# A decoder trunk on one core: the key lookup's small tensors move to the accumulation banks, and the modulation tiles run in quarters

## What is computed

```python
def adaln_params(c, w, b):
    return jnp.split(jax.nn.silu(c) @ w + b, 6, axis=-1)

def peer_ffn(h, w_q, sub_keys, u_tab, v_tab):
    ...
    v1, i1 = lax.top_k(s[:, :, 0], PEER_TOPK)
    v2, i2 = lax.top_k(s[:, :, 1], PEER_TOPK)
    cand = (v1[..., :, None] + v2[..., None, :]).reshape(n, PEER_HEADS, PEER_TOPK * PEER_TOPK)
    cidx = (i1[..., :, None] * PEER_N_KEYS + i2[..., None, :]).reshape(n, PEER_HEADS, PEER_TOPK * PEER_TOPK)
    best, sel = lax.top_k(cand, PEER_TOPK)
    eidx = jnp.take_along_axis(cidx, sel, axis=-1)
    gates = jax.nn.softmax(best, axis=-1)
    ...
```

## Time and profile before

| | us |
|---|---|
| median of 3 runs | 2521.32 |
| lowest, highest | 2515.03, 2521.76 |
| profiled execution, its own time | 2514.56 |
| its span | 2512.7 |
| TensorE busy in the span | 2400.0 |
| VectorE, ScalarE, GpSimd busy | 1419.9, 983.2, 634.3 |

### The profile page before, as it was taken

How to read it: one execution, slowest core, us unless ns; L and a number is a source line. 1 busy time by engine, 2 the same in 40 slices (tenths; PEclk the granted TensorE clock), 3 DMA queues, 4 the chain that set the end, 5 groups by cost and what they waited for, 6 DMA issues and landing times.

```text
span 2512.7 us, 51051 instructions
## 1 busy us (share of the span) xinstructions
PE 2400.0 (96%) x19142; PEld 2185.7 (87%) x19142; DVE 1419.9 (57%) x3306; ACT 983.2 (39%) x1645; POOL 634.3 (25%) x445
## 2 busy tenths in 40 slices
PE   7888999999999999999989977999999999999998
PEld 2478887888889999999978445899999999999998
DVE  6674269577778533333344232269988995333333
ACT  3334433333333344444443131444344434444443
POOL 1015457500000122222254000468500001222222
PEclk8989999999999999999999988999999999999999
DMA  6524455545454454454453663444433334554444
GB/s 246 196 68 152 142 167 187 181 161 168 160 168 143 143 186 162 164 166 167 161 207 117 233 237 136 155 151 159 134 126 126 130 129 135 185 167 165 162 165 144
DMA packets 114871, 405.45 MB, mean 161 GB/s; under 512 B 13275, under 2 KB 13403, under 8 KB 113723
## 3 DMA queue, kind: packets, MB, share of 16 engines
q1 hardware_dynamic: 111048, 388.68, 46.1%
q10 hardware_dynamic: 3699, 15.08, 1.5%
HBM read 394.58 MB, written 9.14 MB: 161 GB/s over the span
## 4 chain that ended last, share of the span: by engine, by line
PE 68%; issue 20%; POOL 9%; DMA 1%; ACT 1%; DVE 1%; POOLq 0%; ACTq 0%; DVEq 0%; SPq 0%
PE ps L1325 11%; PE ps L1329 11%; PE ps L1333 11%; POOL ring_lo L1968 8%; PE ps L1188 7%; PE ps L1189 7%; PE ps L1192 7%; PE ps L1260 5%; PE ps L997 2%; POOL ring_lo L1975 1%; PE ps L755 1%; PE ps L748 1%; PE ps L752 1%; PE ps L1007 1%; PE ps L1046 0%
## 5 line engine op out<-in xcount | busy, mean ns | idle before, releaser
L369 ACT ACTIVATE wt_hi<-ring 128x1024 fp32r<-128x1024 f32 x552 | 580.2, 1051 | 603.6 <-PE ps L1192 414.7
L1921 DVE TENSOR_TENSOR ring_lo<-ring,wt_hi 128x1024 fp32r<-128x1024 f32 x256 | 315.3, 1232 | 496.1 <-ACT wt_hi L369 496.1
L1188 PE MATMUL ps<-split,wt_hi 128*128 128x288 f32 x2048 | 572.7, 305 | 2.9 <-ACT big L420 2.0
L1189 PE MATMUL ps<-split,wt_hi 128*128 128x288 f32 x2048 | 559.5, 297 | 0.0
L1994 POOL TENSOR_TENSOR split<-big,split 128x288 fp32r<-128x288 f32 x256 | 209.8, 820 | 1261.1 <-ACT split L470 662.5
L1188 PEld LDWEIGHTS ps<-split,wt_hi 128*128 128x128 f32 x2048 | 386.5, 189 | 18.6 <-issue 13.3
L1189 PEld LDWEIGHTS ps<-split,wt_hi 128*128 128x128 f32 x2048 | 386.7, 189 | 0.3
L1192 PE MATMUL ps<-split,ring_lo 128*128 128x288 f32 x2048 | 314.6, 296 | 12.6 <-POOL ring_lo L1968 12.6
L1968 POOL TENSOR_TENSOR ring_lo<-ring,wt_hi 128x1024 fp32r<-128x1024 f32 x104 | 285.2, 2750 | 146.9 <-ACT wt_hi L369 146.9
L1325 PE MATMUL ps<-split,wt_hi 128*128 128x288 f32 x2048 | 314.3, 295 | 5.7 <-DVE ada L1635 3.2
L1329 PE MATMUL ps<-split,wt_hi 128*128 128x288 f32 x2048 | 314.3, 295 | 0.0
(11 more groups left out here) (306 smaller groups left out, 2315.1 us busy)
## 6 DMA issues: line engine op xcount, KB each, us to landing
ring<-in_stream SPq DMA_DIRECT2D x680, 512.0 KB, 3.3
big<-in_kc SPq DMA_DIRECT2D x8, 1792.0 KB, 11.9
big<-in_vc SPq DMA_DIRECT2D x14, 1024.0 KB, 7.0
out_qk<-big ACTq DMA_DIRECT2D x1, 3456.0 KB
x_spill<-xT ACTq DMA_DIRECT2D x2, 1152.0 KB, 5.1
big<-x_spill ACTq DMA_DIRECT2D x2, 1152.0 KB, 6.2
out_v<-big ACTq DMA_DIRECT2D x1, 1536.0 KB
xT<-in_xT SPq DMA_DIRECT2D x1, 1152.0 KB, 11.1
```

Of the source, the lines that this page charges most:

```text
L369: nc.scalar.activation(wt_hi[:, n % 2 if b is None else b], ring[:, n % RING], ACT.Copy).then_inc(S["hi_ready"], 1)
L1188: mm(out, w, h_hi[:, c], start=(c == 0), stop=False)
L1189: mm(out, w, h_lo[:, c], start=False, stop=False)
L1921: TT(ring_lo[:, s], ring[:, s], wt_hi[:, s % 2].bitcast(F32), ALU.subtract)\
```

## The change

Lookup: the keys (`keys_ps`) and the candidates' places (`other_ps`) become fp32 in banks 0 to 3, which nobody else uses from the copy of the last scores until `sel_turn`. The bf16 copies `i16` and `selab5` go. The product with the keys then has one input in working memory and one in the banks; the comparison too. The four adds become one `tensor_reduce`.

Modulation: `ada_tile` does four matmuls of 256 columns to partitions 0, 32, 64 and 96, in place of two of 512. `ada_row` copies four pieces of 9 x 256 in place of two of 9 x 512, and `ada_turn` contracts over 128 rows of `gtmp` in place of 64, with eight matmuls as before. Both layers' tiles are changed.

```diff
@@ build @@
+        flat = ps[:, 0:4, :].rearrange("p b n -> p (b n)")
+        other_ps = flat[:, 0:2 * UNITS * 16].rearrange("p (z n) -> p z n", z=2)
+        keys_ps = flat[:, 1024:1024 + 2 * UNITS * 16].rearrange("p (u z a) -> p u z a", u=UNITS, z=2)
@@ ada_row @@
-            nc.scalar.activation(gtmp[0:ROWS, 0:512], ps[0:ROWS, bank, :], ACT.Copy)
-            nc.scalar.activation(gtmp[32:32 + ROWS, 0:512], ps[32:32 + ROWS, bank, :], ACT.Copy).then_inc(S["ada_row"], 1)
+            for z in range(4):
+                r = slice(32 * z, 32 * z + ROWS)
+                ins = nc.scalar.activation(gtmp[r, 0:256], ps[r, bank, 0:256], ACT.Copy)
+            ins.then_inc(S["ada_row"], 1)
@@ ada_tile @@
-                for z in range(2):
-                    ins = mm(ps[32 * z:32 * z + ROWS, bank, :], ccol[:, c * ROWS:(c + 1) * ROWS],
-                             ring[:, n % RING, 512 * z:512 * z + 512], start=(c == 0), stop=(c == NC - 1))
+                for z in range(4):
+                    ins = mm(ps[32 * z:32 * z + ROWS, bank, 0:256], ccol[:, c * ROWS:(c + 1) * ROWS],
+                             ring[:, n % RING, 256 * z:256 * z + 256], start=(c == 0), stop=(c == NC - 1))
@@ ada_turn @@
-                for z in range(2):
-                    for q in range(4):
-                        m = 8 * nb + 4 * z + q
-                        ins = mm(ps[:, bank, m * ROWS:(m + 1) * ROWS], gtmp[0:64, 128 * q:128 * q + 128],
-                                 ident[0:64, 32 * z:32 * z + ROWS], start=True, stop=True)
+                for z in range(4):
+                    for q in range(2):
+                        m = 8 * nb + 2 * z + q
+                        ins = mm(ps[:, bank, m * ROWS:(m + 1) * ROWS], gtmp[:, 128 * q:128 * q + 128],
+                                 ident[:, 32 * z:32 * z + ROWS], start=True, stop=True)
@@ peer_dve @@
-                own(CP(i16, i16u))
+                own(CP(keys_ps, i16u))
...
-                own(CP(selab5, selabu))
-                own.settle()
-                ab, other = selab5[:, 0:2], selab5[:, 2:4]
-
-                own(TS(selab5[:, 2], selab5[:, 2], 12.0, None, ALU.subtract))
-                own.settle()
-                own(TT(other, other, ab, ALU.subtract))
-                own.settle()
-                own(TT(other, other, selab5[:, 4].unsqueeze(1).broadcast_to([P, 2, KU]), ALU.mult))
-                own.settle()
-                own(TT(ab, ab, other, ALU.add))
+                own(TS(other_ps[:, 0], selabu[:, 2], 12.0, None, ALU.subtract))
+                own(CP(other_ps[:, 1], selabu[:, 3]))
+                own.settle()
+                own(TT(other_ps, other_ps, selabu[:, 0:2], ALU.subtract))
+                own.settle()
+                own(TT(other_ps, other_ps, selabu[:, 4].unsqueeze(1).broadcast_to([P, 2, KU]), ALU.mult))
+                own.settle()
+                ab = other_ps
+                own(TT(ab, ab, selabu[:, 0:2], ALU.add))
...
-                    own(TT(e4, e4, i16[:, :, z].unsqueeze(2).broadcast_to([P, UNITS, 16, 16]), ALU.mult))
+                    own(TT(e4, e4, keys_ps[:, :, z].unsqueeze(2).broadcast_to([P, UNITS, 16, 16]), ALU.mult))
                     own.settle()
-
-                    for n in (8, 4, 2):
-                        own(TT(e4[:, :, :, 0:n], e4[:, :, :, 0:n], e4[:, :, :, n:2 * n], ALU.add))
-                        own.settle()
-                    own(TT(sel3[:, z], e4[:, :, :, 0], e4[:, :, :, 1], ALU.add))
+                    own(nc.vector.tensor_reduce(sel3[:, z].rearrange("p u k -> p (u k)"),
+                                                e4.rearrange("p u k a -> p (u k) a"), X, ALU.add))
```

More of the change, by code:

```diff
@@ L167, in build @@
         v16 = rg.take(2 * UNITS * 16).rearrange("p (u z a) -> p u z a", u=UNITS, z=2)
-        i16_f = rg.take(2 * UNITS * 16).bitcast(BF16)
-        i16 = i16_f[:, 0:2 * UNITS * 16].rearrange("p (u z a) -> p u z a", u=UNITS, z=2)
-        iota16 = i16_f[:, 2 * UNITS * 16:2 * UNITS * 16 + 16]
+        iota16 = rg.take(8).bitcast(BF16)
         i16u_f = rg.take(2 * UNITS * 16)
@@ L183, in build @@
         subk = subk_t.rearrange("p (h k) -> p h k", h=PH)
-        selab5 = rg.take(2 * KU + KU // 2).bitcast(BF16).rearrange("p (z n) -> p z n", z=5)
         assert rg.at <= 128 * T - NC * T
```

## The result

The changed kernel takes 2481.92 us in the median (2480.65 to 2484.02, 4 runs), against 2521.28 (2515.03 to 2521.76) before: 0.985 of its time, interval 0.9833 to 0.9867, 39 us less. The forecast was 2473 with a range of 2458 to 2500. A second series, the eleventh experiment, gave 2485.40, ratio 0.9858 (0.9839 to 0.9877).

The account below looks back on a forecast made before the run. TensorE, busy nearly all the span, was taken as the bound. Lookup 16.6, layer 1's tiles 19.2 and the start 10.0 sum to 45.8 us off: 2468.8, or 2475.4 from the median; 2473 was given, range 2458 to 2500.

Parts of the forecast that it names:

- The lookup: In both layers' PEER, the stall between GpSimd and VectorE goes: 16.6 us less, bounds 0 and 17.6.
- the rule of two inputs in working memory: A VectorE operation with two inputs in working memory excludes a GpSimd operation reading there; a `tensor_reduce` never does.
- rival 3: In the lookup, the reduction still excludes GpSimd: the 16.6 us are gone, the tiles' 29 remain, 2492 us; 6%.
- The 1.0 us taken off for hidden waits: Taken from the lookup's 17.6 us for waits of ScalarE and the loads that the stall may hide now.
- VectorE's margin: After the lookup: layer 1's margin grows by 3 us or more; layer 0 had 27.0 us left and keeps most.
- Layer 1's 48 tiles: Modulation tiles inside layer 0's PEER: 0.40 us less each, at most 0.45; 19.2 us in all, bounds 0 and 21.6.
- Rivals 2 and 4: Modulation tiles: 2, four groups overlap no more than two, 2505 us, 8%; 4, groups run one after another, 2568, 4%.
- The start: Layer 0's 48 tiles before S5: 7.0 us sooner at the first S5 product, 3.0 in its loop; 10, bounds 0 and 15.
- the working's 35.8: The lookup's 16.6 us plus 19.2 us from layer 1's 48 modulation tiles.
- Here not every saved 0.4 us reaches the end: Layer 0's tiles before S5, priced group by group for loads, waits and clock, less 1.2 for transfers: 7.0 us sooner.
- rival 1: The kernel's start gives nothing, since TensorE gets half its clock for longer or loads set the pace: 2485 us; 17%.
- its own case: Whole kernel: the forecast's own account, 2458 to 2486 us, given 62%.

Follow-up runs that it names:

- the eleventh experiment: The changed kernel measured once more, nothing altered, beside the kernel before: 2485.40 us, ratio 0.9858.
- experiment 7: Kernel before with the change's lookup in the banks but the four bf16 adds kept, modulation tiles in halves: 2498.78 us, ratio 0.9916.
- The third experiment: The changed kernel with quarters in layer 1's modulation tiles only, layer 0's in halves: 2486.84 us, ratio 0.9868.
- the fourth run: The changed kernel plus zero-weight matmuls in front of seven of layer 0's tiles that wait for loads: 2475.25 us, ratio 0.9826.
- the eighth run: The fourth run plus more zero-weight matmuls, in front of tile 40 and of S5 steps 5, 6 and 7: 2471.35 us, ratio 0.98.
- experiment 12: The eighth run plus zero-weight matmuls in front of TensorE's first tile (80) and tile 4 (84): 2465.77 us, ratio 0.9776.

## Why the prediction was right, and where it was not

**The lookup: right in size and in cause.** 8.9 us in layer 1 and 8.7 in layer 0, and comparison, product and reduction within 0.2 us of their estimates. The banks did all of it (experiment 7: 481.0 us in layer 1 and 47.3 for layer 0's twelve steps, both as with the reduction); the rule of two inputs in working memory, taken from the earlier trace rows, holds in both directions, and rival 3 is gone: the four reductions took 4.95 us each with GpSimd at work beside them. What I had not said is that the reduction is worth nothing beside the banks: alone it gives 1.0 us in layer 1 (and a median 8.2 us lower, which no trace explains), with the banks 0. The 1.0 us taken off for hidden waits was not needed in layer 1. VectorE's margin there was put at 3 us or more and is 12.5: it is through with the lookup at 1751.2 and makes the first `ring_lo` at 1763.7.

**Layer 1's 48 tiles: right, a little low per tile.** From tile 64 to tile 80 sixteen steps take 73.49 us where they took 77.08, with eight modulation tiles: 0.449 us each, and the working's bound was 0.45. That is 21.5 us for 48. Layer 0's PEER as a whole is 27.7 us shorter, which leaves 19 for them beside the lookup's 8.7: some 2.5 us go to other waits. Rivals 2 and 4 fall: four groups of 256 columns run side by side.

**The start: the mis-sized term.** It was put at 10 us. In the two traces it is 2.2 us lost, not won. The medians leave room for 4 us or nothing: 39.4 in the first series and 35.0 in the second, less the 35.7 behind the GLU. But that 35.7 comes from before's fastest execution and from one of two of the change, which are 4.2 us apart there, so that its closeness to the working's 35.8 is in part luck. The third experiment says 1 to 5, within the noise.

The step that failed is "Here not every saved 0.4 us reaches the end", in what it priced: tiles "bound by loads" at 1.5 us, 1.2 us off for the transfers, and the full clock for all that follows. TensorE needed less time per tile and met loads that were not there: it waited 4.1 us in place of 2.6 at the last three, and ran what came next at 1.2 GHz, 6.8 us dearer than at the full clock; from 40 to 52 us it had lost as much, where before lost some 3. That is rival 1, with both its reasons at once, and its 2485 lies nearer to the two series (2481.9, 2485.4) than the forecast's 2473: the range held, since 2485 lies inside what the forecast allowed for its own case (2458 to 2486). I had its half clock in the earlier trace rows and priced it as an alternative, not as a consequence of the saving itself. The working also counted eighteen tiles ahead of 63.66 us, where TensorE's timeline has 22; with them its saving would have been larger still, and further off.

That the waits bring the drop is shown where fill took most of them away: both executions of the change ran at half clock at both places, the fourth run's at full clock, and the eighth run's interval lies wholly under the change's. Not every wait does it: the eighth run dropped to half clock behind waits of 0.9 and 0.2 us, and the fourth passed one of 1.30 at full clock. With fill the quarters give 5.1 us in the median (11.4 at the GLU of the two traces), and with half the bytes 4.7 (2.2 at the GLU), so under 10 in both medians: there TensorE waits 6 to 7 us more for loads with quarters than with halves (11.1 against 5.1, 11.7 against 4.9), because a tile that is done sooner meets a load that is not. The clock and the loads both count, and the runs don't part the one's share from the other's.

**The forecast's checks.** TensorE full at 420 to 450, 4.95 us in both layers and 3.92 us steps came true. A first line-1109 instruction 7 us earlier did not; a TensorE at half clock was named as a sign of error, for 60 to 100 us, and came at 64 to 68 (0.57) and from 100 on. VectorE's margin held: its longest wait behind layer 0's lookup is 30.9 us where it was 27.0.

## What to carry to other kernels

A saving on an engine that waits for loads soon after is not only hidden: the longer wait can cost TensorE its clock for the next stretch (here 6.8 us twice). Price that stretch at half rate before counting the saving, and where it matters fill the wait with work that adds zero. When two engines hold each other, move the operands of the long instructions and leave the short ones: the banks gave everything here, and the neater sum nothing on top of them. Two edits to one stretch are not worth the sum of what each gives alone. Compare the parts of two traces that run unchanged code first; that spread is the smallest difference one execution can show.

## What the runs showed of the hardware that was not expected

The windows' granted clock is not the whole story at the very start. In the changed kernel's first windows PEclk stands at 1.00, yet the eight matmuls of the weights take 7.19 us from 22.10 and four tiles 3.60 from 29.22, the durations that go with 0.50 elsewhere; in the eighth run the same row took 7.19 us with 0.50 beside it. After 7.6 us of zero matmuls in front (experiment 12) the tiles took 1.91. Durations of a known instruction are the safer reading.

How the exclusion shares out depends on who comes first. Under long comparisons and products GpSimd is held (13.4 us for three). Between short adds VectorE is (9.27 us for three), and in experiment 7, where GpSimd is not behind, GpSimd is held 0.8 us at most; before, an instruction of 2.40 us took up to 3.52 under the same adds.

The same code up to the GLU ended between 177.3 and 188.9 us in five profiled executions with layer 0 in halves and no fill, and before's median run lies 7 us above its fastest. Why the clock drops in one execution at a wait that another passes at full clock is open.
